# Stick-breaking attention in a two-block network: values' products by alternating heads, and four attention streams laid differently beside the branches

## The reference, cut to what matters

```
z = q kT * scale
valid = s_pos < t_pos
log_1m = where(valid, log_sigmoid(-z), 0)
log_a = log_sigmoid(z) + reverse_cumsum(log_1m) - log_1m
a = where(valid, exp(log_a), 0)
out = a @ v[:kend]
```

## Time and profile before

| what | value |
|---|---|
| median of three executions | 1701.23 us (1699.09 to 1701.57) |
| the profiled execution's own time | 1700.55 us |
| its span, first to last instruction | 1698.8 us |
| TensorE busy (matmul) | 1678.0 us, 99% of the span |
| VectorE busy | 900.7 us, 53% |
| ScalarE busy | 660.0 us, 39% |
| GpSimd busy | 147.6 us, 9% |
| mean granted TensorE clock | 0.997 |
| share of the chain that ended last, TensorE | 91% |

### The profile page before, as it was taken

The page is one execution under the profiler, slowest core; times in us unless marked ns, Lnnn a source line. Parts: engine busy times, 40 slices in busy tenths (PEclk is TensorE's granted clock), DMA queues, the critical chain, the costliest instruction groups (busy, mean ns, idle before and its releaser), DMA issues.

```text
span 1698.8 us, 19053 instructions
## 1 busy us (share of the span) xinstructions
PE 1678.0 (99%) x7756; PEld 1338.1 (79%) x7756; DVE 900.7 (53%) x1193; ACT 660.0 (39%) x936; POOL 147.6 (9%) x163
## 2 busy tenths in 40 slices
PE   9999999999999999999999999999999999999999
PEld 7877777788888778888888877777666888888887
DVE  5336654455563445444443337867645677777321
ACT  5254343333553333222222335245575444444211
POOL 0000100111110011000000220322111100000000
PEclk9999999999999999999999999999999999999999
DMA  6222222223444122322232222421203222322321
GB/s 259 96 78 75 74 75 80 82 89 101 158 152 133 50 75 87 100 99 92 95 100 99 100 100 87 153 72 63 75 26 111 93 94 100 99 96 92 111 92 57
DMA packets 47462, 164.26 MB, mean 97 GB/s; under 512 B 5056, under 2 KB 5184, under 8 KB 47056
## 3 DMA queue, kind: packets, MB, share of 16 engines
q1 hardware_dynamic: 46192, 158.88, 27.8%
q0 software_dynamic: 896, 3.70, 0.7%
q10 hardware_dynamic: 288, 0.48, 0.1%
HBM read 158.81 MB, written 4.23 MB: 96 GB/s over the span
## 4 chain that ended last, share of the span: by engine, by line
PE 91%; DVE 4%; ACT 3%; issue 1%; DMA 0%; POOL 0%; SPq 0%; DVEq 0%; ACTq 0%; POOLq 0%
PE pst L359 90%; ACT WH L906 1%; ACT L911 1%; PE pst L524 0%; PE pst L796 0%; DVE WL L1522 0%; DMA raw<-wst 0%; DVE XL L1534 0%; DVE scr L2115 0%; DVE qx L1754 0%; ACT Sx L906 0%; POOL acc L2236 0%; ACT ZH L906 0%; ACT misc L906 0%; DVE ML L1530 0%
## 5 line engine op out<-in xcount | busy, mean ns | idle before, releaser
L359 PE MATMUL pst<-XH,WH 128*128 128x512 f32 x1320 | 528.4, 400 | 0.0
L359 PE MATMUL pst<-XH,WL 128*128 128x512 f32 x1320 | 514.9, 390 | 0.0
L359 PE MATMUL pst<-XL,WH 128*128 128x512 f32 x1320 | 514.5, 390 | 0.0
L1522 DVE TENSOR_TENSOR WL<-raw,WH 128x1024 fp32r<-128x1024 f32 x276 | 343.9, 1247 | 319.4 <-ACT WH L906 318.9
L906 ACT ACTIVATE WH<-raw 128x1024 fp32r<-128x1024 f32 (+1 forms) x278 | 291.5, 1049 | 365.8 <-PE pst L359 360.2
L359 PEld LDWEIGHTS pst<-XH,WH 128*128 128x128 f32 x1320 | 248.1, 188 | 64.8 <-issue 14.3
L359 PEld LDWEIGHTS pst<-XL,WH 128*128 128x128 f32 x1320 | 248.3, 188 | 52.3 <-issue 3.4
L359 PEld LDWEIGHTS pst<-XH,WL 128*128 128x128 f32 x1320 | 248.0, 188 | 52.4
L359 PE MATMUL pst<-HH,WH 128*128 128x512 f32 x352 | 136.9, 389 | 0.0
L359 PE MATMUL pst<-HL,WH 128*128 128x512 f32 x352 | 136.9, 389 | 0.0
L359 PE MATMUL pst<-HH,WL 128*128 128x512 f32 x352 | 136.9, 389 | 0.0
(11 more groups left out here) (249 smaller groups left out, 1832.6 us busy)
## 6 DMA issues: line engine op xcount, KB each, us to landing
raw<-wst SPq DMA_DIRECT2D x276, 512.0 KB, 3.4
X<-xT SPq DMA_DIRECT2D x7, 512.0 KB, 7.6
xs<-X SPq DMA_DIRECT2D x1, 2048.0 KB, 8.9
nC<-cd POOLq DMA_DIRECT2D x4, 512.0 KB, 8.2
X<-xs SPq DMA_DIRECT2D x2, 1024.0 KB, 5.6
outT<-X SPq DMA_DIRECT2D x8, 256.0 KB, 4.3
qx<-memT SPq DMA_DIRECT2D x1, 1024.0 KB, 5.0
gt<-cd POOLq DMA_DIRECT2D x1, 1024.0 KB, 4.9
```

The source lines that it names most:

```text
L359: return nc.tensor.matmul(out, lhs, rhs, start=start, stop=stop)
L1522: vec.tensor_tensor(WL[:, i % NHL, :], raw[:, i % NRAW, :], WH[:, i % NHL, :].bitcast(F32), ALU.subtract).then_inc(wl, 1)
```

## The change

```diff
--- before.py
+++ after.py
@@ -304,7 +304,7 @@
         mixer_order = weave(
-            {"main": (0, 1, mixer_steps), "stick00": (0.02, 0.5, 20), "stick01": (0.5, 0.97, 20), "stick10": (0.04, 0.53, 20), "stick11": (0.53, 1.0, 20)},
+            {"main": (0, 1, mixer_steps), "stick00": (-0.0593, 0.481, 20), "stick01": (0.577, 0.996, 20), "stick10": (-0.0412, 0.676, 20), "stick11": (0.65, 1.01, 20)},
             {("stick01", 0): (("stick00", 20),), ("stick11", 0): (("stick10", 20),)})
@@ -526,9 +526,9 @@
-                    for e in range(2):
-                        h = 2 * pt + e
-                        for j in range(i + 1):
+                    for j in range(i + 1):
+                        for e in range(2):
+                            h = 2 * pt + e
                             ins = mm(ps[b0][64 * e:64 * e + 64, 0:P], v[:, j, h * 64:(h + 1) * 64], pb[:, s, e, j * P:(j + 1) * P], j == 0, j == i)
```

## The result

The changed kernel takes 1691.41 us (median of 4, 1690.78 to 1692.6) against 1700.99 us of the kernel before on the same chip: a ratio of 0.9946 with a 95% interval of 0.9929 to 0.9964, or 9.6 us less (6.1 to 12.1 by that interval). The forecast was 8.3 us less, 1692.9 us.

The account below looks back on a forecast made before the run. TensorE, at 91% of the span, was taken as the bound. The terms -3.0 - 4.9 - 1.7 + 1.0 + 0.3 = -8.3 us gave a median of 1692.9 us from 1701.23, range 1689.5 to 1698.5.

Parts of the forecast that it names:

- Alternating the heads: Values' products in the first block's mixer: blocks of 4 and 3 key blocks shorten to 1.03 and 0.81 us, -3.0 us.
- Waits: TensorE's waits in the first block's mixer all go with the new layout: -4.9 us, bounds 0 and 5.4.
- clock: The 3.4 us at half speed around the end of the mixer's longest wait go: -1.7 us, bounds 0 and 1.7.
- More excursions: Attention work between tile passes costs 0.34 us per change-over; 41 excursions instead of 38: +1.0 us, bounds 0.6 and 1.5.
- The rule: Trainium skill on array tiling: changing the tiling mode drains TensorE, changing only the tile does not.
- New waits: Attention chains with short lead, at the start and in the second half, make TensorE wait: +0.3 us, bounds 0 and 3.
- the waits only move: Rival, chance 0.12: the mixer's 4.9 and 1.7 us come back elsewhere; 1699.2 us, no measurable change.
- The clock falls anyway: Rival, chance 0.15: the stretch from 85 to 96 is still mostly short passes; one fall costs 1.7 us, giving 1694.6.
- Alternating brings nothing: Rival, chance 0.08: in the values' products the halves share a bank and TensorE overlaps by itself; 1695.9 us.
- slower: Rival, chance 0.04: VectorE's chain in the mixer's second half delays every transpose; at 1.9 us each the time is 1708.

Follow-up runs that it names:

- the run with the later copy: Kernel before with ScalarE's copies of the spatial results one place later, behind the attention's copy to q: 1697.71 us (10 runs), ratio 0.9984.
- the second edit alone: Kernel before with only the heads alternating, streams laid as before: 1697.84 us (10 runs), ratio 0.9986.
- the run with half products: Changed kernel plus 24 products with 64 columns of weights, half of the array, in attention steps empty on TensorE: 1703.92 us, one execution.

## Why the prediction was right, point by point

The forecast was 1.3 us short of the measured gain. That is inside the interval of the measurement; the two profiled executions, 9.8 us apart, are what the terms can be held against.

- *Alternating the heads*, -3.0: the blocks came out at 1.02 and 0.80 us, where 1.03 and 0.81 were forecast. Alone it measured -2.4 us, -2.6 at HH. The sign that was named beside it, 5 passes in flight from the start, did not come: it was 4 at 0.15 us.
- *Waits*, -4.9, and *clock*, -1.7: both are gone entirely from the trace. The layout alone measured -5.9 us, -6.5 at HH, and the run with the later copy gave 3.4 us at HH for the one wait of 2.15 with its fall, near the 2.15 + 1.7 that the sum had for it. The clock's 1.7 us are the least sure of the sum: the profiled execution of before belongs to those with a mean clock of 0.997, and the shorter ones may lack a fall anyway, as the prediction itself allowed. That so much of it was there to be won in the measured median of before (1700.99 us) was in part luck. For the waits in the second spatial stretch and the first one for `pb`, the run with the layout alone shows that the new places remove them; which queue position made each of them is not shown.
- *More excursions*, +1.0: this is the term that was mis-sized. I gave 0.34 us to every excursion alike and counted three more. Grouping the trace by what stands in each excursion, 12 before and 14 after hold transposes alone, which cost next to nothing beside their passes, and the stretches of half products (64 rows or 64 columns of weights), which do change the division of the array, are 29 in both. The price itself was right, 0.34 us for a half product, but only there; a whole one cost 0.03. The term should have been about 0. The rule was quoted in the prediction beside the term, and not applied in it: transposes use the whole array. That is the larger part of the 1.3 us by which the kernel beat the forecast.
- *New waits*, +0.3: no row among the waits. At the start the chunk was made from 77.80 us, where 78.1 was forecast, and the transposes came at 86.37 (86.3). The place that the sums gave as 0.1 us late, the transposes at 154, shows it (timeline of TensorE, changed kernel):

```profile
296.04 0.40 PE L359 MATMUL pst<-ZH,WL 128*128 128x512 f32 x1
296.35 0.88 PE L524 MATMUL pst<-cm,sg 128*128 128x128 f32 x6
```

The distance is 0.31 us where it is 0.23 for the other transposes: late by 0.08. Adding up a chain against the steps of TensorE was good to a tenth of a microsecond there.

Of the rivals, *the waits only move* did not come true in the mixer, though it did for every edit tried in the second block. *The clock falls anyway* did not either; there was no fall in the mixer in any of the ten profiles with the 2.15 us wait removed, and one in both that have it. *Alternating brings nothing* fell with the run of the second edit alone, *slower* with the result.

## What to carry to other kernels

In kernels where all engines follow one written order, look for the wait whose releaser is an engine that was itself idle: its step may be queued behind one that waits for a third engine, as here for 2.15 us, and moving one position can be worth the wait and the clock's fall behind it. Then look at what the moved step meets, for in a stretch without room the wait turns up again one step later. Products that use halves of the array should alternate after four passes at most (four in a row cost 0.05 us here, six 0.27), and what costs is going over to halves and back (0.34 us here), not leaving the tile's work as such.

## What I had not expected of the hardware

Executions of one program differ by where and how long the clock is down. Behind the single wait of 2.15 us (with short passes around it) the clock fell in both profiles that have it; in the run with the later copy, waits of 1.2 and 1.1 us remained and no fall came with them. In the second block a wait of 2.35 us stands beside 6.8 us at 1.2 GHz in eight profiles and beside 3.4 us in one, the run with half products, though its waits there (2.35 and 1.12 us) are those of the run with the second edit alone; waits of 4.36 and 6.28 us stand beside 10.2 and 13.7 us. The changed kernel's second profile has its first and last pass of `HH` here:

```profile
L359 PE MATMUL pst<-HH,WH x352: 389/389/389, 878.0 to 1685.6; 128*128 128x512 f32 x176
```

That is 0.1 us behind the first profile at the first pass and 0.6 at the last, with the kernel the same. So what an edit seems to win or lose in one block of one trace, by a microsecond or so, need not be the edit's. Several executions, and their mean clock beside the time, tell more than the trace of one of them.
